# One-hot buffers of the gate spreading stage laid out token by token, with indices and gates stored in pairs

## The reference

```python
s1 = einsum('thd,nd->thn', q[..., :128], keys1)      # 8 heads, 128 keys
s2 = einsum('thd,nd->thn', q[..., 128:], keys2)
v1, i1 = top_k(s1, 16);  v2, i2 = top_k(s2, 16)
# the 16 best sums v1 + v2 of each head, their expert i1 * 128 + i2, and softmax gates
idx  = ...   # (T, 8 * 16) experts, 16384 = 128 * 128 in all
gate = ...   # (T, 8 * 16)
act = gelu(einsum('tkd,td->tk', u_tab[idx], x)) * gate
out = einsum('tk,tkd->td', act, v_tab[idx])
```

## Time and profile before

| what | value |
|---|---|
| median of 3 runs | 2665.53 us (2664.76 to 2665.78) |
| span of the profiled execution, first to last instruction | 2666.5 us |
| PE busy | 2474.5 us, 93% of the span |
| DVE busy | 1717.8 us, 64% |
| ACT busy | 1480.5 us, 56% |
| POOL busy | 758.7 us, 28% |
| mean granted clock of PE, as a share of 2.4 GHz | 0.880 |

### The profile page before, as it was taken

One profiled execution on the slowest core, in us unless ns is written; L12 is line 12 of the kernel. 1 busy time (PEld: TensorE's weight loads), 2 busy tenths in 40 slices (PEclk: granted clock), 3 DMA queues, 4 the chain that ended last, 5 costly groups with the idle time before them and its releaser, 6 DMA issues.

```text
span 2666.5 us, 54657 instructions
## 1 busy us (share of the span) xinstructions
PE 2474.5 (93%) x18850; PEld 1865.7 (70%) x18850; DVE 1717.8 (64%) x3306; ACT 1480.5 (56%) x2644; POOL 758.7 (28%) x590
## 2 busy tenths in 40 slices
PE   1577899999999999999988999999999999999998
PEld 1456677777765568888866656777777555788887
DVE  8897599974445555555545557999444555555555
ACT  3222588885553335555578447888755433455554
POOL 4982179990000000000037205799400000000000
PEclk6796999999985569999999759999999655999999
DMA  2000445555530025555554124455555000555553
GB/s 70 4 0 21 127 135 174 172 168 181 177 113 0 0 63 178 176 180 175 180 198 134 48 100 124 150 173 165 182 175 179 15 0 0 159 179 176 178 178 123
DMA packets 88940, 328.79 MB, mean 123 GB/s; under 512 B 10784, under 2 KB 10784, under 8 KB 88480
## 3 DMA queue, kind: packets, MB, share of 16 engines
q1 hardware_dynamic: 88272, 318.36, 38.2%
q0 software_dynamic: 592, 9.47, 0.9%
HBM read 321.60 MB, written 6.19 MB: 123 GB/s over the span
## 4 chain that ended last, share of the span: by engine, by line
PE 41%; issue 38%; POOL 13%; DVE 6%; ACT 1%; POOLq 0%; DVEq 0%; DMA 0%; SPq 0%; ACTq 0%
POOL wsp L255 11%; PE ps L297 9%; PE ps L298 9%; PE ps L299 9%; PE ps L1347 5%; DVE big L815 2%; DVE big L804 1%; PE ps L1332 1%; PE ps L1807 1%; PE ps L1333 1%; PE ps L903 1%; DVE big L563 1%; PE ps L1785 1%; PE ps L362 1%; PE ps L1053 1%
## 5 line engine op out<-in xcount | busy, mean ns | idle before, releaser
L244 ACT ACTIVATE wsp<-ring 128x512 f16<-128x512 f32 x1200 | 752.0, 629 | 651.4 <-PE ps L299 631.9
L257 DVE SCALAR_TENSOR_TENSOR wsp<-ring,wsp 128x512 f16<-128x512 f32 x784 | 541.2, 692 | 541.4 <-ACT wsp L244 541.4
L297 PE MATMUL ps<-hs,wsp 128*128 128x288 f16 x2752 | 795.5, 289 | 44.7 <-POOL wsp L255 23.9
L298 PE MATMUL ps<-hs,wsp 128*128 128x288 f16 x2752 | 794.8, 289 | 0.0
L299 PE MATMUL ps<-hs,wsp 128*128 128x288 f16 x2752 | 794.5, 289 | 0.0
L298 PE MATMUL ps<-hT,wsp 128*128 128x288 f16 (+2 forms) x2560 | 639.4, 263 | 0.0
L297 PE MATMUL ps<-hT,wsp 128*128 128x288 f16 (+2 forms) x2560 | 618.4, 263 | 6.0 <-DVE hT L1391 6.0
L255 POOL TENSOR_TENSOR wsp<-ring,wsp 128x512 f16<-128x512 f32 x416 | 562.8, 1380 | 198.0 <-ACT wsp L244 197.5
L299 PE MATMUL ps<-hT,wsp 128*128 128x288 f16 (+2 forms) x2560 | 617.8, 262 | 0.0
L297 PEld LDWEIGHTS ps<-hs,wsp 128*128 128x128 f16 x2752 | 270.8, 98 | 146.5 <-POOL wsp L255 46.8
L299 PEld LDWEIGHTS ps<-hs,wsp 128*128 128x128 f16 x2752 | 271.8, 99 | 71.0
(11 more groups left out here) (252 smaller groups left out, 2700.4 us busy)
## 6 DMA issues: line engine op xcount, KB each, us to landing
ring<-in_v SPq DMA_DIRECT2D x256, 512.0 KB, 3.5
ring<-in_ua SPq DMA_DIRECT2D x144, 512.0 KB, 3.5
ring<-in_ub SPq DMA_DIRECT2D x112, 512.0 KB, 3.5
ring<-in_wq SPq DMA_DIRECT2D x32, 512.0 KB, 3.5
ring<-in_win SPq DMA_DIRECT2D x32, 512.0 KB, 3.5
ring<-in_glu SPq DMA_DIRECT2D x16, 512.0 KB, 3.6
big<-in_hgs POOLq DMA_DIRECT2D x1, 4096.0 KB, 13.9
ring<-in_wout SPq DMA_DIRECT2D x8, 512.0 KB, 3.7
```

What stands on the lines that cost most here:

```text
L244: nc.scalar.activation(wsp[:, k % 2, 0, cols], ring[:, k, cols], ACT.Copy, scale=scale).then_inc(hi_ready, 1)
L257: nc.vector.scalar_tensor_tensor(out=lo, in0=w, scalar=SC, in1=hi, op0=ALU.mult, op1=ALU.subtract).then_inc(lo_dve, 1)
L297: nc.tensor.matmul(out, w_hi, hi, start=start, stop=False, **kw)
L298: nc.tensor.matmul(out, w_hi, lo, start=False, stop=False, **kw)
```

## The change

The one-hot buffers are laid out [token t, key j], so that the 128 values of a token lie side by side. For that, `iota_r` becomes a single run of 128 numbers, which the instructions repeat over tokens; the two difference banks hold four tokens each, where they held 64 keys each; the second matmul of a difference repeats each token's index over 128 columns. `i2T` and the gates are stored twice, side by side, so that DVE can read a pair of equal values at neighbouring addresses (d = 2) and repeat the pair over 64 pairs of keys. The multiplication with the gates is split in two instructions, one for the high and one for the low half of the gate, and `poh` counts by two. `hot2` of x = 0 moves from `hT` to a new buffer `spare2`.

```diff
-        iota_r = sb("iota_r", [P, NK, GT], F16)
+        iota_r = sb("iota_r", [P, NK], F16)
...
-            return flat.rearrange("p (j t) -> p j t", t=GT)
+            return flat.rearrange("p (t j) -> p t j", t=GT)
...
-            g = ps[:, 2, 0:T]
+            g = ps[:, 2, 0:T, None].to_broadcast([P, T, 2])
             L_(vv.tensor_scalar(gate_hi, g, SC, None, ALU.mult))
...
-            for m, (dst, sign) in enumerate(((neg_i1T, -1.0), (i2T, 1.0))):
-                vv.tensor_scalar(dst, ps[:, m, 0:T], sign, None, ALU.mult).then_inc(ptc[L], 1)
+            vv.tensor_scalar(neg_i1T, ps[:, 0, 0:T], -1.0, None, ALU.mult).then_inc(ptc[L], 1)
+            vv.tensor_copy(i2T, ps[:, 1, 0:T, None].to_broadcast([P, T, 2])).then_inc(ptc[L], 1)
...
+        def pairs(a):
+            return a.rearrange("p t (j d) -> p t j d", d=2)
...
-                    v.wait_ge(poh[L], i * 2 + x - 1)
-                vv.tensor_tensor(hot2[x], iota_r[:, :, :], of_tokens(i2T, i, x), ALU.is_equal).then_inc(pe2[L], 1)
+                    v.wait_ge(poh[L], 2 * (i * 2 + x) - 2)
+                sh = [P, GT, NK // 2, 2]
+                vv.tensor_tensor(pairs(hot2[x]),
+                                 iota_r[:, :].rearrange("p (j d) -> p j d", d=2)[:, None].to_broadcast(sh),
+                                 i2T[:, tokens(i, x), None, :].to_broadcast(sh), ALU.is_equal).then_inc(pe2[L], 1)
...
-                sh = [P, 2, NK, GT]
-                vv.tensor_tensor(hot2g[x], hot2[x][:, None].to_broadcast(sh),
-                                 gates[:, :, None, ds(i * (2 * GT) + x * GT, GT)].to_broadcast(sh),
-                                 ALU.mult).then_inc(poh[L], 1)
+                sh = [P, GT, NK // 2, 2]
+                for f in range(2):
+                    vv.tensor_tensor(pairs(hot2g[x][:, f]), pairs(hot2[x]),
+                                     gates[:, f, tokens(i, x), None, :].to_broadcast(sh), ALU.mult).then_inc(poh[L], 1)
...
-                    nc.tensor.matmul(out, ident_h[:, :], iota_r[:, b * nh:(b + 1) * nh, :], start=True, stop=False)
-                    mm = nc.tensor.matmul(out, ident_h[:, :],
-                                          of_tokens(neg_i1T, i, x)[:, 0:nh, :], start=False, stop=True)
+                    t0 = ds(i * (2 * GT) + x * GT + b * half, half)
+                    nc.tensor.matmul(out, ident_h[:, :], iota_r[:, None, :].to_broadcast([P, half, NK]),
+                                     start=True, stop=False)
+                    mm = nc.tensor.matmul(out, ident_h[:, :], neg_i1T[:, t0, None].to_broadcast([P, half, NK]),
+                                          start=False, stop=True)
...
-                        mm = nc.tensor.matmul(out, hot1[x][:, :, s], hot2g[x][:, f, :, s], start=(f == 0), stop=(f == 1))
+                        mm = nc.tensor.matmul(out, hot1[x][:, s, :], hot2g[x][:, f, s, :], start=(f == 0), stop=(f == 1))
```

More of the change, by code:

```diff
@@ L143, in build @@
         hT_half = hT[:, :, :].rearrange("p c t -> p (c t)").bitcast(F16)
-        neg_i1T, i2T, gate_hi, gate_lo = (hT_half[:, T * k:T * k + T] for k in range(4))
-        gates = hT_half[:, 2 * T:4 * T].rearrange("p (f t) -> p f t", f=2)
+        neg_i1T = hT_half[:, 0:T]
+        i2T = hT_half[:, T:3 * T].rearrange("p (t d) -> p t d", d=2)
+        gates = hT_half[:, 3 * T:7 * T].rearrange("p (f t d) -> p f t d", f=2, d=2)
+        gate_hi, gate_lo = (gates[:, f] for f in range(2))
         asp = hT[:, 3:5, :].rearrange("p a t -> p (a t)").bitcast(F16).rearrange("p (s f t) -> p s f t", s=2, f=2)
@@ L154, in spread_buffer @@
             flat = (hs_half[:, n * k:n * k + n] if k < 4 else
-                    hT_half[:, 4 * T + n * (k - 4):4 * T + n * (k - 4) + n])
-            return flat.rearrange("p (j t) -> p j t", t=GT)
+                    hT_half[:, 7 * T + n * (k - 4):7 * T + n * (k - 4) + n])
+            return flat.rearrange("p (t j) -> p t j", t=GT)
         hot1 = [spread_buffer(k) for k in range(2)]
-        hot2g = [a.rearrange("p (f j t) -> p f j t", f=2, t=GT) for a in
-                 (hs_half[:, 2 * NK * GT:4 * NK * GT], hT_half[:, 4 * T:4 * T + 2 * NK * GT])]
+        hot2g = [a.rearrange("p (f t j) -> p f t j", f=2, t=GT) for a in
+                 (hs_half[:, 2 * NK * GT:4 * NK * GT], hT_half[:, 7 * T:7 * T + 2 * NK * GT])]
         spare = sb("spare", [P, NK * GT // 2])
-        hot2 = [spread_buffer(6), spare[:, :].bitcast(F16).rearrange("p (j t) -> p j t", t=GT)]
+        spare2 = sb("spare2", [P, NK * GT // 2])
+        hot2 = [a[:, :].bitcast(F16).rearrange("p (t j) -> p t j", t=GT) for a in (spare2, spare)]
         small = sb("small", [P, 256])
@@ L1262, in spread_loop, with tokens @@
                 body(GROUPS // 2 - 1, 1, False, last=True)
-        def of_tokens(a, i, x):
-            return a[:, None, ds(i * (2 * GT) + x * GT, GT)].to_broadcast([P, NK, GT])
+        def tokens(i, x):
+            return ds(i * (2 * GT) + x * GT, GT)
+        def pairs(a):
+            return a.rearrange("p t (j d) -> p t j d", d=2)
         def peer_g_act(act, L):
@@ L1274, in body @@
                     act.wait_ge(pG[L], i * 2 + x - 1)
-                nc.scalar.activation(hot1[x].rearrange("p j t -> p (j t)"),
+                nc.scalar.activation(hot1[x].rearrange("p t j -> p (t j)"),
                                      ps[:, 4 + 2 * x:6 + 2 * x, :].rearrange("p b n -> p (b n)"),
@@ L1328, in difference @@
                     pe.wait_ge(pab[L], i * 2 + x - 1)
-                nh = NK // 2
+                half = GT // 2
                 for b in range(2):
                     out = ps[:, 4 + 2 * x + b, :]
-                    nc.tensor.matmul(out, ident_h[:, :], iota_r[:, b * nh:(b + 1) * nh, :], start=True, stop=False)
-                    mm = nc.tensor.matmul(out, ident_h[:, :],
-                                          of_tokens(neg_i1T, i, x)[:, 0:nh, :], start=False, stop=True)
+                    t0 = ds(i * (2 * GT) + x * GT + b * half, half)
[3 more added lines that the diff above has]
+                                          start=False, stop=True)
                 mm.then_inc(pdf[L], 1)
@@ L1342, in body @@
                 pe.wait_ge(phA[L], i * 2 + x + 1)
-                pe.wait_ge(poh[L], i * 2 + x + 1)
+                pe.wait_ge(poh[L], 2 * (i * 2 + x) + 2)
                 for s in range(GT):
@@ L1861, in _ @@
             L_(nc.gpsimd.memset(epsc[:, :], EPS))
-            L_(nc.gpsimd.iota(iota_r[:, :, :], pattern=[[1, NK], [0, GT]], base=0, channel_multiplier=0,
+            L_(nc.gpsimd.iota(iota_r[:, :], pattern=[[1, NK]], base=0, channel_multiplier=0,
                               allow_small_or_imprecise_dtypes=True))
```

## The result

The changed kernel takes 2484.86 us (median of 4 runs, 2483.61 to 2485.08), the one before 2665.66 us in the same session (median of 4). The ratio is 0.9312 with a 95% interval of 0.9298 to 0.9325: 180.8 us less, where 163.8 us were forecast. The time lies 1.1 us under the low end of the range.

A forecast was written before the change was run, and what follows sets the result against it. PE alone was taken to bound the spreading stage, at 5.41 us a group. With 3.1 us a group, layer 0's stage falls from 191.88 to 110.0 us, 163.8 us saved over two layers: 2502 us, range 2486 to 2542 us.

The forecast's parts named there:

- G matmuls: PE, spreading stage: contiguous operands cut a 128-column matmul from 0.233 us to 0.107 at half clock, 0.053 to 0.078 at full.
- Difference matmuls: PE, four in a group: count, columns and cost stay, 1.68 us at clock 0.50, 0.87 us at 1.00.
- DVE: Spreading stage: `mul` 1.14 us plus three instructions of 0.60 us, 2.94 us for a group, against 2.88 before.
- ACT: Spreading stage: 2.1 us for a group, unchanged, nowhere the bound.
- Gates: Lines 1199 to 1203: three copies double, 0.3 us more each, 0.9 us for a layer, hidden; 1.3 us in all without cover.
- Which engine, then?: Spreading stage: PE bounds at 3.39 us at clock 0.50, DVE at about 3.0 us at 1.00; expected 3.1 us a group.
- The 0.06 us allowed for DVE's address rows: DVE, each group: allowance for extra address rows, which run while the engine computes.
- A second, smaller term of the sum: Layer 0's stage: 35 periods of 3.1 us, last G 1.3 us, 0.23 us to `mul`: 110.0 us instead of 191.88.
- The first: Rival: G matmuls slow for another reason, such as PSUM adds or weight loads; they stay at 0.233 us, 2665 us; 5%.
- The first half of the second: Rival: DVE falls to one element per cycle on pairs, 4.56 us a group, 2604 us; 9% for both halves.
- The other half: Rival: the repeated index costs PE like strided reading, 4.42 us a group at 0.50, 2595 us; 9% for both halves.
- the third: Rival: DVE restarts reading every two elements, 2.28 us per pair instruction, 7.98 us a group, 2844 us; 3%.

The follow-up runs named there:

- experiment 1: Kernel before, only the weights of the G matmuls read contiguously, moving operand still at a step of 8 (wrong G): 2657.77 us, one run.
- experiment 2: Kernel before, only the moving operand of the G matmuls read contiguously, weights still at a step of 8 (wrong G): 2485.74 us.
- Experiment 4: Kernel before, both operands of the G matmuls read at a step of 4 elements instead of 8 (wrong G): 2485.10 us, one run.
- experiments 8: Changed kernel with three more DVE comparisons of 512 elements in each group, to slow DVE: 2576.88 us, one run.
- experiment 9: Changed kernel with five more DVE comparisons of 512 elements in each group, to slow DVE: 2641.13 us, one run.
- experiment 11: Changed kernel with one merged gate multiplication of 2048 elements, POOL multiplying 2 of each group's 8 tokens: 2491.19 us, ratio 0.9336.

## Why the prediction was right, and where it was wrong

**G matmuls.** Forecast: 0.053 to 0.078 us each at full clock. Measured: 0.056 us. That both operands had a step of 8 was named as the suspect; experiments 1 and 2 show that it is the moving one, all but 0.006 us. The rule of the Trainium skill (page "SBUF — State Buffer", section "Door 1: The DMA port swizzle"), that one can stride for free by up to 8 bf16, goes with what the weights show (0.227 against 0.233 us). For TensorE's moving operand the measurements contradict it: 0.233 and 0.117 us at 16 and 8 bytes, against 0.056 us at 2. The prediction took the lines and that limit from the note. The same note says that an access that crosses to a new line of 16 bytes pays a penalty and that a line wants at least two hits; at a step of 16 bytes each line has one hit, so this half of it had the slow reads right. It has the step of 8 bytes wrong, which has two hits and still costs twice the time.

**Difference matmuls.** Forecast: the present cost, the step of 0 free. Right: 0.215 us from start to start at full clock, in the timelines above (825.10 to 825.32).

**DVE.** Forecast: 0.60 us for each instruction on pairs, 1.14 for `mul`, 2.94 us for a group. Measured: 0.60, 0.60, 0.60 and 1.13, in all 2.937 us, averaged over the loop.

**ACT.** Hidden, as forecast: 1.02 and 1.06 us of a period of 2.93.

**Gates.** Forecast: 0.3 us more for each of three copies. They take 0.75, 0.76 and 0.75 us instead of 0.45, and the weight split behind them still waits 0.22 us for ACT, as in the earlier trace rows. Hidden.

**The step that failed** is the end of "Which engine, then?": "I expect that the clock is high for most of the stage, with some stretches at 0.50, and a group at 3.1 us." The direction, the mechanism and the engine that binds were right; the size of a period was not. There was no stretch at 0.50: the clock is 1.00 in every group, with PE busy for 52.23 of 80 us. With PE that fast, its clock has no way to lengthen the period, and the group takes DVE's own 2.937 us. The 0.06 us allowed for DVE's address rows isn't to be seen either. That term is 35 periods x 0.163 us x 2 layers = 11.4 us too long.

**A second, smaller term of the sum** took all 35 periods as equal. At the stage's start the first groups have no `mul`, so G follows G by 2.00 and 2.29 us (778.89, 780.89, 783.18), and the last group has no `equal`. The last G and the way to `mul` were put at 1.3 + 0.23 us, and take 1.09 us (879.50 to 880.59). At the measured period the formula gives 104.3 us from the first G to the last `mul`; it is 101.7 us. That is 2.6 us in each layer, 5.2 us. With both terms the forecast gain of 163.8 us becomes 180.4 us; measured are 90.17 + 90.19 = 180.4 us in the two stages, and 180.8 us between the medians.

**The range** reached down to a period of 2.94 us, 2490 us, and the measured period is that one; the size of the period alone would have left the time inside. The 5.2 us for the ends of the stage took it out: for them and for the clock behind the stage the range had allowed 4 us at its low end.

**The rivals.** The first (G slow for another reason) is excluded by experiment 2: with only the reading step of one operand changed, the same matmuls with as many loads and sums in PSUM take 0.064 to 0.065 us. The first half of the second didn't happen, but it is real: without pairs DVE's instructions do fall to 1.13 us for 1024 elements, and the kernel takes 2603 us, where that rival said 2604. The other half (a repeated index costs PE) and the third (2.28 us for each instruction on pairs) show nowhere.

**What stays open.** Why the clock fell in the kernel before within the first group and stayed at 0.50 isn't settled. Experiment 4 keeps PE's records gapless too, at 1.00; experiments 8 and 9 show that a slow pace gives a clock that changes, not one that stays at half. It could be the pace and the strided stream together; no run separates the two at an equal pace. The nearest pair is experiment 1 (strided, 5.31 us, 0.50 throughout) and experiment 9 (contiguous, 5.11 us, 0.71 and 0.83). It is open, too, which property of `mul` spares it from POOL: it reads PSUM, but it also works on float32 and has only one source in SBUF.

## What to carry to other kernels

When a matmul's records show more time per column than one cycle at either clock, look at the step of its moving operand first, and lay that buffer out so that its inner dimension is contiguous, or nearly so (a step of 4 bytes cost 0.001 to 0.002 us of 0.056 here); the weights can keep their step. When a value is repeated along the inner dimension of a 2-byte operation with two sources on DVE, store it twice and read it in pairs. When POOL is to take work from a bound DVE, put it beside an instruction of DVE like `mul`, which reads PSUM, and make it short enough to end, with its semaphore, inside that instruction.

## What the runs showed of the hardware

The cost of a strided moving operand doesn't depend on TensorE's clock: 0.233 us for 128 columns at 0.50 and at 1.00. For 8, 4 and 2 bytes it is 0.117, 0.057 to 0.058 and 0.056 us at 1.00. It hardly falls on the weights (0.006 us with the moving operand strided, 0.008 to 0.009 us with it contiguous).

A 2-byte instruction of DVE with two SBUF sources that started 0.70 us before the end of one of POOL's went from 0.68 to 1.25 us; one in float32 of the same 1024 elements that reads PSUM stayed at 1.21 to 1.22 us. POOL needs 2.16 us for 1024 float16 elements, 1.04 for 512 and 0.61 for 256. From the end of a DVE instruction to the start of the POOL instruction that waits for it, and back, it takes about 0.2 us each way (experiment 11: 841.81 to 842.01, and 843.05 to 843.23).

Two DVE instructions of 1024 elements take 1.20 us from start to start, one of 2048 takes 1.14 us: an instruction costs about 0.06 us by itself.
